# Norm weights applied while the high and low parts of the input are written, x in four transfers, first squares on two engines

## What is computed

```python
def rms_norm(x, gain):
    xf = x.astype(jnp.float32)
    inv = lax.rsqrt(jnp.mean(xf * xf, axis=-1, keepdims=True) + NORM_EPS)
    return (xf * inv).astype(x.dtype) * gain

for l in range(DEPTH):
    x = x + 0.5 * swiglu(rms_norm(x, ffn1_norm[l]), ffn1_wg[l], ffn1_wu[l], ffn1_wd[l])
    h = rms_norm(x, mix_norm[l])
    z = h @ w_in[l]
    ...
    x = x + jnp.concatenate([attn_out, conv_out], axis=-1) @ w_out[l]
    x = x + 0.5 * swiglu(rms_norm(x, ffn2_norm[l]), ffn2_wg[l], ffn2_wu[l], ffn2_wd[l])
return rms_norm(x, final_norm)
```

## Time and profile before

| | us |
|---|---|
| median of 3 runs | 1254.76 |
| the 3 runs | 1251.52, 1254.76, 1254.94 |
| the profiled execution | 1248.0 |
| its span, first to last instruction | 1246.2 |
| PE busy in the span | 1210.2 (97%) |
| DVE busy | 820.1 (66%) |
| ACT busy | 656.4 (53%) |
| POOL busy | 169.2 (14%) |

### The profile page before, as it was taken

The page is one execution under the profiler, slowest core; times in us unless marked ns, Lnnn a source line. Parts: engine busy times, 40 slices in busy tenths (PEclk is TensorE's granted clock), DMA queues, the critical chain, the costliest instruction groups (busy, mean ns, idle before and its releaser), DMA issues.

```text
span 1246.2 us, 27436 instructions
## 1 busy us (share of the span) xinstructions
PE 1210.2 (97%) x10050; PEld 1170.8 (94%) x10050; DVE 820.1 (66%) x1388; ACT 656.4 (53%) x1121; POOL 169.2 (14%) x228
## 2 busy tenths in 40 slices
PE   6999999999999999999999999999998999998998
PEld 6999999999999999999999999999996887998888
DVE  6777665867666655777655867767656666645764
ACT  5555543646444544555544546555445666646652
POOL 3000000351000000000010451000000000401960
PEclk9999999999999999999999999999997999999999
DMA  7655754445555654556754335556652430543542
GB/s 281 200 197 196 233 172 140 143 136 189 182 188 196 225 167 131 192 193 206 231 173 140 133 134 193 200 187 212 226 166 69 135 130 6 177 146 138 175 145 85
DMA packets 56742, 210.91 MB, mean 169 GB/s; under 512 B 7200, under 2 KB 9280, under 8 KB 56544
## 3 DMA queue, kind: packets, MB, share of 16 engines
q1 hardware_dynamic: 54048, 203.45, 49.0%
q0 software_dynamic: 2480, 6.48, 1.8%
q10 hardware_dynamic: 144, 0.06, 0.0%
HBM read 208.91 MB, written 1.05 MB: 168 GB/s over the span
## 4 chain that ended last, share of the span: by engine, by line
PE 92%; DVE 4%; ACT 2%; issue 2%; DMA 0%; DVEq 0%; ACTq 0%; SPq 0%
PE bank L1149 27%; PE bank L1151 26%; PE bank L1150 26%; PE bank L1187 2%; PE bank L1492 2%; DVE w_lo L735 1%; DVE h_lo L754 1%; PE bank L1472 1%; ACT w_hi L452 1%; PE bank L1457 1%; PE bank L1394 1%; PE bank L1396 1%; PE bank L1395 1%; PE bank L1452 1%; DVE h L748 1%
## 5 line engine op out<-in xcount | busy, mean ns | idle before, releaser
L1149 PE MATMUL bank<-h_hi,w_hi 128*128 128x256 f32 (+1 forms) x1992 | 565.8, 284 | 17.1 <-DVE w_lo L735 11.7
L1151 PE MATMUL bank<-h_hi,w_lo 128*128 128x256 f32 (+1 forms) x1992 | 556.1, 279 | 0.0
L1150 PE MATMUL bank<-h_lo,w_hi 128*128 128x256 f32 (+1 forms) x1992 | 555.9, 279 | 0.0
L735 DVE TENSOR_TENSOR w_lo<-w_raw,w_hi 128x1024 fp32r<-128x1024 f32 (+1 forms) x360 | 466.0, 1296 | 79.8 <-ACT w_hi L452 79.2
L452 ACT ACTIVATE w_hi<-w_raw 128x1024 fp32r<-128x1024 f32 (+1 forms) x360 | 397.7, 1108 | 91.4 <-PE bank L1151 69.3
L1149 PEld LDWEIGHTS bank<-h_hi,w_hi 128*128 128x128 f32 x1992 | 376.1, 189 | 25.9 <-issue 21.1
L1151 PEld LDWEIGHTS bank<-h_hi,w_lo 128*128 128x128 f32 x1992 | 378.6, 190 | 0.0
L1150 PEld LDWEIGHTS bank<-h_lo,w_hi 128*128 128x128 f32 x1992 | 376.3, 189 | 0.9
L1149 PE MATMUL bank<-g_hi,w_hi 128*128 128x256 f32 x832 | 231.4, 278 | 0.5 <-DVE x_res L920 0.5
L1151 PE MATMUL bank<-g_hi,w_lo 128*128 128x256 f32 x832 | 230.9, 278 | 0.0
L1150 PE MATMUL bank<-g_lo,w_hi 128*128 128x256 f32 x832 | 230.9, 278 | 0.0
(11 more groups left out here) (160 smaller groups left out, 1214.9 us busy)
## 6 DMA issues: line engine op xcount, KB each, us to landing
w_raw<-in_w SPq DMA_DIRECT2D x296, 512.0 KB, 3.3
w_raw<-in_wd SPq DMA_DIRECT2D x64, 704.0 KB, 4.1
w_raw<-in_relbias POOLq DMA_DIRECT2D x64, 64.0 KB, 2.3
btab_sb<-in_btab POOLq DMA_DIRECT2D x1, 1536.0 KB, 9.9
x_res<-in_xT SPq DMA_DIRECT2D x2, 512.0 KB, 4.9
out_T<-x_res SPq DMA_DIRECT2D x8, 128.0 KB, 1.7
rope_sb<-in_rope POOLq DMA_DIRECT2D x1, 272.0 KB, 3.5
mats_sb<-in_mats POOLq DMA_DIRECT2D x1, 192.0 KB, 3.7
```

The costliest lines, as they stand in the source:

```text
L735: dve.tensor_tensor(wlo[:, slot, 0:cols], raw[:, slot, 0:cols], whi[:, slot, 0:cols].bitcast(F32), ALU.subtract).then_inc(lo_ready[slot], 1)
L1149: pe.matmul(o, h, xh, start=first, stop=False)
L1150: pe.matmul(o, h, xl, start=False, stop=False)
L1151: return pe.matmul(o, lo, xh, start=False, stop=last)
```

## The change

The scaled copy h goes. ACT reads x and multiplies by the norm's weight while it writes h_hi (its scale operand is a column of `sml`, one number a partition). DVE computes x·weight − h_hi in one instruction with two inputs. ACT's `high` no longer waits for DVE's h. In `down` and `wout` ACT now does high first and the square after it. At the start x comes in four transfers; ACT squares the even tiles and DVE the odd ones; ACT waits for the norm's weights (`g_loaded`), and the first splits stand after other tiles. POOL's wait before its loads of constants is for h_lo of tile 7 instead of h. The second block's norm is as it was.

```diff
-        x_loaded = [sem(f"x_loaded{p}") for p in range(2)]
+        x_loaded = [sem(f"x_loaded{p}") for p in range(KT // 2)]
...
-            for p in range(2):
-                half = slice(p * KT // 2, (p + 1) * KT // 2)
-                sp.dma_start(x[:, half, 0:T], xT[:, half]).then_inc(x_loaded[p], 16)
+            for p in range(KT // 2):
+                two = slice(2 * p, 2 * p + 2)
+                sp.dma_start(x[:, two, 0:T], xT[:, two]).then_inc(x_loaded[p], 16)
...
-            pool.wait_ge(h32_done, KT)
+            pool.wait_ge(h_lo, KT)
...
-            def high(q, k, slot):
-
-                act.wait_ge(h32_done, q * KT + k + 1)
-                act.activation(hhi[:, bass.ds(k * HS, T)], h32[:, slot, 0:T], ACT.Copy).then_inc(h_hi, 1)
+            def high(q, k):
+
+                act.activation(hhi[:, bass.ds(k * HS, T)], x[:, k, 0:T], ACT.Copy,
+                               scale=sml[:, bass.ds(q * KT + k, 1)]).then_inc(h_hi, 1)
...
+                            act.wait_ge(x_ready[p], q * 4 + o2 + (PRIME - 3))
                             act.wait_ge(acc_step, q * 7 + o2 * 2 + p - 1)
-                            act.wait_ge(x_ready[p], q * 4 + o2 + (PRIME - 3))
+                            high(q, o2 * 2 + p)
                             square(p, x[:, o2 * 2 + p, 0:T])
-                            high(q, o2 * 2 + p, p)
...
+                    high(q, o)
                     square(o % 2, x[:, o, 0:T])
-                    high(q, o, o % 2)
...
+            act.wait_ge(g_loaded, 16)
             for k in range(KT):
-                act.wait_ge(x_loaded[k // (KT // 2)], 16)
-                if k >= 2:
-                    act.wait_ge(acc_step, k - 1)
-                square(k % 2, x[:, k, 0:T])
-                high(0, k, k % 4)
-                if k in (3, 5, 7):
-                    split((k - 3) // 2, PT8, uses0(1))
+                act.wait_ge(x_loaded[k // 2], 16)
+                if k % 2 == 0:
+                    if k >= 2:
+                        act.wait_ge(acc_step, k - 1)
+                    square(0, x[:, k, 0:T])
+                high(0, k)
+                if k in (2, 5, 7):
+                    split((2, 5, 7).index(k), PT8, uses0(1))
...
-            def scaled(q, k, slot):
-
-                dve.tensor_scalar(h32[:, slot, 0:T], x[:, k, 0:T], sml[:, bass.ds(q * KT + k, 1)], None, ALU.mult)\
-                   .then_inc(h32_done, 1)
-
-            def low(q, k, slot):
+            def low(q, k):
+
                 dve.wait_ge(h_hi, q * KT + k + 1)
                 h = bass.ds(k * HS, T)
-                dve.tensor_tensor(hlo[:, h], h32[:, slot, 0:T], hhi[:, h].bitcast(F32), ALU.subtract)\
-                   .then_inc(h_lo, 1)
+                dve.scalar_tensor_tensor(out=hlo[:, h], in0=x[:, k, 0:T], scalar=sml[:, bass.ds(q * KT + k, 1)],
+                                         in1=hhi[:, h].bitcast(F32), op0=ALU.mult, op1=ALU.subtract).then_inc(h_lo, 1)
...
-            for k in range(KT + 1):
-                if k < KT:
-                    dve.wait_ge(x_loaded[k // (KT // 2)], 16)
-                    scaled(0, k, k % 4)
-                if k > 0:
-                    low(0, k - 1, (k - 1) % 4)
-                if k in (4, 6, 8):
-                    split((k - 4) // 2, PT8, uses0(1))
+            for k in range(KT):
+                dve.wait_ge(x_loaded[k // 2], 16)
+                if k % 2:
+                    if k >= 2:
+                        dve.wait_ge(acc_step, k - 1)
+                    dve.tensor_tensor(sq[:, 1, 0:T], x[:, k, 0:T], x[:, k, 0:T], ALU.mult).then_inc(sq_done[1], 1)
+                low(0, k)
+                if k in (3, 6, 7):
+                    split((3, 6, 7).index(k), PT8, uses0(1))
```

## The result

The changed kernel took 1258.88 us (median of 22 runs, 1253.88 to 1266.29), the kernel before 1253.67 in the same job (22 runs, 1240.87 to 1268.20). The ratio is 1.0061, 95% interval 1.0038 to 1.0084: slower. The means, 1258.9 against 1253.2, differ by 5.7 us (0.45%). The forecast was 1253.5 with a range up to 1257.5; the time lies above it. The profiled execution after took 1255.38, against 1248.0 before: +7.4.

What follows compares the result with a forecast made beforehand. PE bounds the kernel (92% of the chain), and its pace decides most. Start −0.3, `wout` −0.9 and −0.5, last `down` +0.45 sum to −1.25, taking the median 1254.76 to 1253.5 us; range 1245.0 to 1257.5.

Steps and rivals of the forecast that it cites:

- I read the median as an execution with two slow parts: Feed-forward parts: median 1254.76 holds two at 117.3 ns a matmul, not 112.8, 7.0 us each; the profiled 1248.0 holds one.
- The rule itself: Behind `wout`: waits shrink or vanish; if `sum_norm` without a wait leaves the slow pace, both second feed-forwards are slow.
- 1246.75 + 7.0: Profiled execution: 1246.75 if paces fall as before, plus 7.0 for one more slow part, 1253.75, near the median's 1253.5.
- a first feed-forward falling slow: Rival: at the start, `sum_norm` passes without a wait or in another phase, adding 7.0 us, 1260.5; chance 14%.
- Start: First tiles: weights land at 8.2, w_lo starts at 10.1, PE at 11.6, no wait before tile 6; −0.3 us (−1.2 to +1.0).
- `wout`: DVE's cycle per output falls from 2.83 to 2.63 us, below PE's 2.71; −0.9 in layer 1, −0.5 in layer 2.
- End of the last `down`: h_hi now stands ahead of ACT's square, so the square and the final norm come later; +0.45 us.
- the 76 ns that the sum used: ACT's h_hi at the last `down`: a column operand takes 0.494 us against 0.418 with immediates, from the trace.
- The gap between the layers: Between first and second layer PE stands 2.44 us, blamed on h_lo; its first matmul needs only tile 0, so left alone.

Runs made afterwards that it cites:

- experiment 2: The kernel before with the change made in `wout` alone (weights applied in h_hi and h_lo, no scaled copy, h_hi ahead of the square): mean 1257.8 us, ratio 1.0074.
- experiment 4: The changed kernel with x in two transfers again, all else as after: mean 1261.5 us (9 runs), ratio 1.0094 to the kernel before.

## Why the prediction was wrong

**The step that failed** is "I read the median as an execution with two slow parts", and with it that the median's count of slow parts was a constant of the kernel, to which the change's effect could be matched. The rule itself was seen: "if the slow pace follows a `sum_norm` without a wait, both second feed-forwards are slow". It was then taken to mean 1246.75 + 7.0, as though the first feed-forwards stayed fast. What the runs show in its place: the kernel before draws all four, with 1.6 slow on average and runs from 1239 to 1269; the change fixes two of the four at slow and leaves the other two drawn. From an all-fast 1241 that is 1241 + 14.1 + the slow ones among the two first parts (14 of 36 in the profiles, 2 · 14/36 · 7.0 = 5.5) = 1260.6; 1258.9 was measured, so this is an estimate with 1.7 us left over. Before: 1241 + 1.6 · 7.0 = 1252; 1253.2 measured in its job (mean). Three runs between 1251.5 and 1254.9, beside a profile at 1248.0, had shown one step of a ladder of five. The chance that I gave to a slower result (14%) hung on a first feed-forward falling slow. That happens, and as I described it, behind a `sum_norm` without a wait; but it happens with the start of the kernel before as well (experiment 2, whose start is unchanged, has it), so it isn't what the change added. The profiled execution itself came as the rule said, with both second feed-forwards slow and 1255.38 against 1253.75.

**Start**, −0.3 predicted (−1.2 to +1.0), +0.65 measured at PE's pace. The chain was right (weights, h_hi, h_lo, w_lo), the landing was the mis-sized term: 9.2, not 8.2, though the bytes ahead were the same (experiment 4: 8.4 with two transfers). w_lo's 1.76 beside POOL added 0.5 that the sum had left out. The later w_lo meant no wait before tile 6, as said.

The prediction took from the Trainium skill, "SBUF — State Buffer", section "Who interferes with whom", that DVE and GpSimd exclude each other when a DVE instruction with two SBUF inputs meets a GpSimd one that reads SBUF. The traces agree, and here the one that begins second is stretched: w_lo 1.76 behind an addition of 0.72 that had begun first, and 1.23 where w_lo had begun first.

**`wout`**, −0.9 and −0.5 predicted. DVE's cycle fell to 2.48, by 0.35 where 0.20 was forecast; the fused h_lo was 0.01 dearer, not 0.07. Layer 2 shows 1.4 and layer 1 0.2; at equal paces that is about 0.9 and 0.8 (above). Right in mechanism, about right in size. What was meant as the gain, that PE no longer waits, is what cost the 7 us.

**End of the last `down`**, +0.45 predicted, +0.51 measured. A column operand made h_hi 507 ns on average against 418 for a like one with immediates: +89.

The Trainium skill, "ScalarE: Activation LUTs", section "What ACT_TABLE_LOAD costs", has 93 ns for a column operand; these rows agree with it better than the 76 ns that the sum used.

**The gap between the layers** was left alone and stayed: 2.73 us from start to start at 478.15 after, 2.71 at 477.58 before.

## What to carry to other kernels

Look at the spread and the steps of single run times before costing a change, and at more than three runs: where the same program falls on steps of a fixed height, find what the step is, and ask of a change which of the draws it fixes, not only what it takes off the path. A wait of less than 0.1 us that is "worth removing" can be the thing that lets a following stage run at its better pace. Here, in the changed kernel, it paid to put a late operation (`sum_norm`) where PE has to wait a little for another engine: 12 us better than the same kernel without. In the kernel before, whose small waits were still there, the same move gave nothing that can be told.

## What was not expected of the hardware

PE at a granted clock of 1.00 has two exact sustained paces for the same stream of 128x256 matmuls with 128x128 weights: 113.33 and 117.78 ns from start to start, each held unchanged through a whole feed-forward part, some 180 us and 1500 matmuls, in all 72 parts of the 18 traces. The pace changed only at gaps. Gaps at which PE waited for another engine left either; those without a wait behind `wout` left the slow one in 12 of 12. Ahead of the first feed-forwards, a `sum_norm` begun at the lower clock left the fast one in 10 of 10, without an experiment on it (the one such case with PE's wait for itself was slow). Why PE falls into one or the other no run here shows. Nor do the changed kernel's own 22 runs stand on the steps as clearly as those of before (18 of them fill 1254 to 1261 evenly); that, too, is open.
